# Two gated stages of a hybrid backbone: a weight remainder is computed amid the convolution's taps, and two roots are taken ahead of an evacuation

## The chip, the cores and the metric

One core of a Trainium2 chip runs the whole kernel in one launch. The metric is the device time in microseconds (us) of that core. The engines of the core are TensorE (PE in the rows; PEld are its weight loads), VectorE (DVE), ScalarE (ACT), GpSimd (POOL) and SyncE (SP, which here only issues DMAs). Each runs its own queue of instructions in order, and semaphores tie the queues together.

## The reference, cut to what matters

The program computes two layers of a backbone on 1024 latent and 256 context tokens with 1024 channels. The change touches only the front of layer 0, the gated pointwise unit and the depthwise convolution behind it:

```python
def conformer_conv(h, w_in, b_in, dw_w, dw_b, ln_g, ln_b, w_out, b_out):
    a, gt = jnp.split(h @ w_in + b_in, 2, axis=-1)
    z = a * jax.nn.sigmoid(gt)
    z = depthwise_conv(z, dw_w, dw_b)          # 31 taps, centred
    z = jax.nn.silu(layer_norm(z, ln_g, ln_b))
    return z @ w_out + b_out
...
a = rms_norm(h, norm_g[i, 0]) * (1.0 + sc1) + sh1     # the input, also for context
y = conformer_conv(a, *cm)
h = h + g1 * rms_norm(y, norm_g[i, 1])
```

After it come a gated feed-forward part with a 3-tap convolution, windowed attention and a second feed-forward part.

## The kernel before

Channels lie on the 128 partitions (8 tiles of 128 channels), tokens along the free dimension. Every weight tile of 1024 x 128 is a "unit" of the stream `wstream`. SyncE loads it into `raw`, ScalarE writes its high part `w_hi` (`split` on ScalarE, L496), VectorE the remainder `w_lo = raw - w_hi` (`split` on VectorE, L1001), and TensorE multiplies three times per tile: high by high, high by low, low by high (`unit`, L1729). There are two slots, j = 0 and 1, and two units make a pair q. I write (q,j) for a unit. A unit of the gated stages is 8 tiles x 3 products x 2 halves of the tokens = 48 matmuls.

Two gated phases (`kind == "glu"`) follow each other: pairs 0 to 7 take the first 660 tokens, pairs 8 to 15 the other 620. In each pair, unit (q,0) gives the channel tile `a`, unit (q,1) the gate. ScalarE evacuates the first to `ug` (L645) and the sigmoid of the second to `uv` (L666), VectorE multiplies them into `zA` and `zB` (the product, L1330), which counts `glu_done`. ScalarE may overwrite `ug` only when the product before is done.

Between units TensorE runs adaptive rows, which compute the shifts, scales and gates of both layers: `ada_turn` (L1766) and `ada_rows` (L1758), 16 + 4 short matmuls on a 1 MB slot that GpSimd loads. ScalarE copies each row out (`ada_row_out`, L503).

The order on each engine is written out by hand. For one pair q = q0 + i before the change:

- ScalarE: evacuate (q,0); high part of (q+1,0), which must wait for unit (q,0) since it overwrites its weights; a hosted root, if any; row out; sigmoid of (q,1); high part of (q+1,1); row out.
- VectorE: wait for the sigmoid; product; remainders of (q+1,0) and (q+1,1); then `conv(n)`, the next n operations of the 31-tap depthwise convolution of 8 tiles (L1013, L1015, L1025, L1028, and L1022 that joins even and odd taps), with n from the lists `CONV_A` and `CONV_B`; then the steps of a hosted norm.
- TensorE: unit (q,0), adaptive rows, unit (q,1), adaptive rows. It starts a unit when its remainder is there and its PSUM slot is evacuated.

Each phase hosts a norm of other work. The first hosts the input norm of the second token chunk (`pre`): squares in pair 0, three sums on VectorE behind pair 1's taps (L1040), average on TensorE ahead of unit (3,0) (L1737), root on ScalarE in pair 3 (L514), reciprocal on VectorE behind pair 3's taps (L1044), normalized tiles behind pair 4's (L1070), then high parts and remainders of the activations in pair 7 (L543, L1076). The second hosts the layer norm of the convolution's first 644 outputs (`ln`): sums behind pair 12's taps (L1212, L1208), average ahead of unit (14,0), mean and centring in pair 13 on VectorE (L1217, L1223), squares, sums behind it, average ahead of unit (15,0), root in pair 15, reciprocal behind pair 14's taps, normalized tiles (L1281), silus in pair 15 (L659), high parts and remainders. TensorE, after the first unit of such a pair, waits for the root before it goes on, since the average shares its PSUM banks with the adaptive sums. Behind pair 15 the output projection of the module (`cm`, pairs 16 to 19) runs.

In the loops of VectorE and of this text i counts pairs within a phase. The product of pair q is called product q. On VectorE what the trace shows behind product q up to product q+1 is pair q's share.

Of the kernel before, what the change touches and what calls it, by code (L numbers as in the profile page):

```python
# [37 lines left out]
GA, MIX, HALF, MIX1 = 660, 644, 640, 516  # L38
GB, MIXB = TOK - GA, TOK - MIX
# [3 lines left out]
ZB = ZC + CTX + PAD  # L43
CB = ZC + CTX - PAD
LAG = 5
N_GROUPS = NB * NKV
N_HEADS = N_GROUPS * QPK
CONV_A = (20, 16, 21, 16, 14, 21, 21, 17)
CONV_B = (22, 22, 22, 22, 23, 9, 10, 14)
# [126 lines left out]
def backbone(nc, xT, wstream, adastream, vec, consts, bconsts, rope, out):  # L176
    ph, n_pairs, pair_tiles = plan()
    assert len(pair_tiles) == n_pairs
    with ExitStack() as ctx:
# [305 lines left out]
        def _(act):  # L485
# [26 lines left out]
            def root(s, w, bank=4):  # L512
                act.wait_ge(norm_step, s)
                A(two(rms[:, 0:w], w), misc(w, bank), ACT.Sqrt, bias=eps_t[:]).then_inc(norm_step, 1)  # L514
# [95 lines left out]
            for x in ph:  # L610
                if "hosted" in x:
                    continue
                kind, q0, s, ch = x["kind"], x["q"], x["s"], x.get("chunk")
# [23 lines left out]
                if kind == "glu":  # L637
                    w, host = ch["n"], x["host"]
                    n = host["n"]
                    for i in range(8):  # L640
                        q, g, ga = q0 + i, x["g"] + i, x["ada"] + 2 * i
                        if g:
                            act.wait_ge(glu_done, g)
                        act.wait_ge(unit_done, 2 * q + 1)
                        A(parted(ug[:, 0:w], w), slot(0, w), ACT.Identity, bias=col("cmb_in", i)).then_inc(evacuated, 1)  # L645
                        split(q + 1, 0)
                        if host["kind"] == "pre" and i == 3:
                            root(host["s"] + 5, GB)
                        if host["kind"] == "ln" and i == 6:
                            act.wait_ge(norm_step, host["s"] + 6)  # L650
                            A(t_mix[:], zA[:, :, 0:MIX], ACT.Square).then_inc(norm_step, 1)
                        if host["kind"] == "ln" and i == 7:
                            root(host["s"] + 11, MIX)
                        ada_row_out(ga)
                        if host["kind"] == "ln" and i == 7:
                            for m in range(4):
                                act.wait_ge(in_normed, 4 * n + m + 1)
                                for k in (2 * m, 2 * m + 1):
                                    last = A(t_mix[:, k], zA[:, k, 0:MIX], ACT.Silu, scale=col("ln_g", k), bias=col("ln_b", k))  # L659
                                last.then_inc(in_modulated, 1)  # L660
                        act.wait_ge(unit_done, 2 * q + 2)
                        tiles = t_gb if host["kind"] == "pre" else t_mix
                        if i == 7:
                            for m in range(2):
                                high_part(n, m, tiles[:, 2 * m:2 * m + 2])
                        A(parted(uv[:, 0:w], w), slot(1, w), ACT.Sigmoid, bias=col("cmb_in", 8 + i)).then_inc(evacuated, 1)  # L666
                        if i == 7:
                            for m in range(2, 4):
                                high_part(n, m, tiles[:, 2 * m:2 * m + 2])
                        split(q + 1, 1)  # L670
                        ada_row_out(ga + 1)
                        if host["kind"] == "pre" and i == 0:
                            pre_squares(host)
                        if host["kind"] == "pre" and i in (5, 6):
                            for m in range(2 * (i - 5), 2 * (i - 4)):
                                modulate(n, m, t_gb[:, 2 * m:2 * m + 2], 0, 0, GA)
# [20 lines left out]
                if kind == "wo":  # L697
# [7 lines left out]
                    for v in range(2 * KT):  # L705
                        q, j, u = q0 + v // 2, v % 2, v % KT
# [26 lines left out]
                if kind == "ffn":  # L733
# [4 lines left out]
                    q, p, d = x["q"], x["p"], x["d"]  # L738
                    head, tail, ln, join = x.get("head"), x.get("tail"), x.get("ln"), x.get("join")
                    final = x.get("last")  # L740
                    narrow = head and "narrow" in head
                    for gi, (f0, nf) in enumerate(groups):
# [75 lines left out]
                        q, p = q + nf, p + nf  # L818
# [58 lines left out]
                if kind == "qkv":  # L877
# [19 lines left out]
                    for t in range(30):  # L897
                        q, j = q0 + t // 2, t % 2
# [45 lines left out]
                if kind == "attn":  # L944
# [17 lines left out]
                    for c in range(cuts_by(-1)):  # L962
                        cut(c)
                    for n in range(N_HEADS + LAG):
                        g, hh, m = n // QPK, n % QPK, n - LAG
                        if m >= 0:
# [24 lines left out]
        def _(dve):  # L991
# [3 lines left out]
            def split(q, j):  # L995

                if isinstance(q, int) and q >= n_pairs:
                    return
                dve.wait_ge(hi_ready, 2 * q + j + 1)
                nt = tiles_of_pair(q)  # L1000
                TT(w_lo[:, j, 0:nt], raw[:, j, 0:nt], w_hi[:, j, 0:nt].bitcast(F32), ALU.subtract).then_inc(lo_ready, 1)  # L1001
# [28 lines left out]
            def conv(n):  # L1030

                for op in range(conv_at[0], min(conv_at[0] + n, 2 * KT * (CW + 1))):
                    conv_tap(op // (CW + 1), op % (CW + 1))
                    conv_at[0] = op + 1
# [249 lines left out]
            for x in ph:  # L1284
                if "hosted" in x:
                    continue
                kind, q0, s, ch = x["kind"], x["q"], x["s"], x.get("chunk")
# [25 lines left out]
                if kind == "glu":  # L1313
                    host = x["host"]
                    pre, n, hs = host["kind"] == "pre", host["n"], host["s"]
                    tiles = t_gb if pre else t_mix
                    if pre:
                        parts = [(zA, PAD, 0, GA - 1), (zB, 0, ZB0, GA)]
                        dve.wait_ge(pad_set, 1)
                    else:  # L1320
                        parts = [(zB, GA - ZB0, 0, LAT - GA), (zB, ZC, LAT - GA, GB)]
                    for i in range(8):
                        q = q0 + i
                        if i == 7:
                            split(q + 1, 0)
                            for m in range(2):
                                remainder(n, m, tiles[:, 2 * m:2 * m + 2])
                        dve.wait_ge(evacuated, 2 * q + 2)
                        for z, zo, lo, hi in parts:
                            last = TT(z[:, i, zo:zo + hi - lo], ug[:, lo:hi], uv[:, lo:hi], ALU.mult)  # L1330
                        last.then_inc(glu_done, 1)
                        if i == 7:
                            for m in range(2, 4):
                                remainder(n, m, tiles[:, 2 * m:2 * m + 2])
                        else:
                            split(q + 1, 0)
                        split(q + 1, 1)
                        if not pre and i == 5:
                            ln_mean_out(hs + 4, MIX)
                            ln_centre(hs + 5, zA, MIX)  # L1340
                        if not pre and i == 1:
                            modulation(0, 16, 48, ADA_B, 2)
                        conv((CONV_A if pre else CONV_B)[i])
                        if pre and i == 1:
                            sum_tiles(hs + 1, t_gb)
                        if pre and i == 3:
                            invert(hs + 6, GB)
                        if pre and i == 4:
                            for m in range(4):
                                pre_normed(host, m)  # L1350
                        if not pre and i == 4:
                            assert conv_at[0] >= KT * (CW + 1)
                            ln_first_sum(hs)
                        if not pre and i == 5:
                            sum_tiles(hs + 7, t_mix)
                        if not pre and i == 6:
                            invert(hs + 12, MIX)
                            for m in range(4):
                                ln_normed(hs + 13, zA, MIX, m)
                if kind == "cm":  # L1360
                    for v in range(KT):
                        q, j = q0 + v // 2, v % 2
# [16 lines left out]
                if kind == "wo":  # L1379
# [8 lines left out]
                    for v in range(2 * KT):  # L1388
                        q, j, u = q0 + v // 2, v % 2, v % KT
# [21 lines left out]
                if kind == "ffn":  # L1411
# [4 lines left out]
                    head, tail, ln, join = x.get("head"), x.get("tail"), x.get("ln"), x.get("join")  # L1416
# [4 lines left out]
                    q, p, d = x["q"], x["p"], x["d"]  # L1421
                    for gi, (f0, nf) in enumerate(groups):
# [84 lines left out]
                        q, p = q + nf, p + nf  # L1507
# [57 lines left out]
                if kind == "qkv":  # L1565
# [45 lines left out]
                    for t in range(30):  # L1611
                        q, j = q0 + t // 2, t % 2
# [44 lines left out]
                if kind == "attn":  # L1657
# [11 lines left out]
                    for c in range(cuts_by(-1)):  # L1669
                        cut(c)  # L1670
                    for n in range(N_HEADS + LAG + 2):
                        g, hh, g_out = n // QPK, n % QPK, (n - LAG - QPK - 1) // QPK
                        if g_out >= 0 and (n - LAG - 1) % QPK == 0:
# [424 lines left out]
```

## Time and profile before

| | us |
|---|---|
| median of 3 runs (2950.06 to 2951.52) | 2951.47 |
| the profiled execution's own time | 2953.52 |
| its span from first to last instruction | 2951.70 |
| TensorE matmuls busy, whole span | 2730.4 (93%) |
| VectorE busy, whole span | 2065.3 (70%) |
| ScalarE busy, whole span | 1285.0 (44%) |
| GpSimd busy, whole span | 132.9 (5%) |
| the gated stages, first product to the end of the last remainder | 75 to 409 |

The shares over the whole span are averages over stages of different kinds: the gated stages are a ninth of it. For a change in one stage the busy times of that stage and the waits in it are what to read. In the rows, "[1.75 <-DVE w_lo L1001]" behind an instruction means that its engine was idle for 1.75 us before it and that the named result released it. Instructions of the same line are merged into one row with their count. The time of a merged row can overlap the next row's start by about 0.1 us, so the difference of two starts is the time that an instruction holds its engine.

### The profile page before, as it was taken

The page shows a single profiled execution, that of the slowest core. Times are in us where ns is not written, and L with a number is a line of the kernel's source. Part 1 is how long each engine was busy: PE and PEld are TensorE (multiplying, and loading weights), DVE is VectorE, ACT ScalarE, POOL GpSimd, SP SyncE. Part 2 cuts the span into 40 slices and gives each one's busy share as a digit, 9 for nine tenths or more (in the row PEclk, how much of TensorE's full clock was granted, in tenths as well). Part 3 has the DMA queues.
Part 4 walks back from the last instruction along what each step waited for, and adds up shares of the span by engine and source line. Part 5 has one row for each costly group of instructions (what it writes and reads, how often), then busy time and mean ns, then how long its engine had stood idle before and what let it go on. Part 6 is the DMA issues. An engine that isn't in the chain of part 4 may idle for free. (4 is left out here: it accounts for less than half of the span.)

```text
span 2951.7 us, 45016 instructions
## 1 busy us (share of the span) xinstructions
PE 2730.4 (93%) x17388; PEld 2462.6 (83%) x17388; DVE 2065.3 (70%) x2897; ACT 1285.0 (44%) x1910; POOL 132.9 (5%) x177
## 2 busy tenths in 40 slices
PE   5898877999999989999999989998999999999996
PEld 4787776999998979999997767776889989778785
DVE  3899988889877367556667767665577457584665
ACT  3232244433436353333443557776453334443333
POOL 0000000000000000000000003333000000000000
PEclk7999988999999989999999989999999999999998
DMA  6444432233232212222222220000222232333322
GB/s 266 147 153 157 143 114 96 69 91 92 75 89 69 72 58 78 87 93 78 86 79 93 79 72 1 2 1 2 79 85 88 92 100 86 100 103 111 100 93 85
DMA packets 66519, 263.14 MB, mean 89 GB/s; under 512 B 6960, under 2 KB 7216, under 8 KB 60080
## 3 DMA queue, kind: packets, MB, share of 16 engines
q1 hardware_dynamic: 58368, 213.17, 22.9%
q0 software_dynamic: 5760, 41.95, 4.1%
q10 hardware_dynamic: 2224, 5.69, 0.6%
q8 instruction: 118, 1.93, 0.3%
q14 instruction: 49, 0.40, 0.0%
HBM read 256.58 MB, written 4.19 MB: 88 GB/s over the span
## 5 line engine op out<-in xcount | busy, mean ns | idle before, releaser
L1729 PE MATMUL PS<-a_hi,w_hi 128*128 128x322 f32 (+7 forms) x3584 | 919.5, 325 | 72.6 <-DVE a_lo L1076 37.5
L1729 PE MATMUL PS<-a_lo,w_hi 128*128 128x322 f32 (+7 forms) x3584 | 899.4, 320 | 0.0
L1729 PE MATMUL PS<-a_hi,w_lo 128*128 128x322 f32 (+7 forms) x3584 | 898.6, 319 | 0.0
L1729 PEld LDWEIGHTS PS<-a_hi,w_hi 128*128 128x128 f32 x3584 | 613.0, 192 | 125.8 <-issue 47.5
L1729 PEld LDWEIGHTS PS<-a_lo,w_hi 128*128 128x128 f32 x3584 | 615.3, 192 | 26.7 <-issue 4.8
L1729 PEld LDWEIGHTS PS<-a_hi,w_lo 128*128 128x128 f32 x3584 | 612.7, 192 | 24.4
L1001 DVE TENSOR_TENSOR w_lo<-raw,w_hi 128x1024 fp32r<-128x1024 f32 (+2 forms) x380 | 443.7, 1171 | 190.9 <-ACT w_hi L496 186.9
L496 ACT ACTIVATE w_hi<-raw 128x1024 fp32r<-128x1024 f32 (+2 forms) x380 | 386.3, 1017 | 0.3 <-DMA raw<-wstream 0.2
L1729 PE MATMUL PS<-z_hi,w_hi 128*128 128x320 f32 (+1 forms) x1056 | 301.2, 340 | 30.1 <-DVE z_lo L1426 27.9
L1729 PE MATMUL PS<-z_hi,w_lo 128*128 128x320 f32 (+1 forms) x1056 | 298.7, 337 | 0.0
L1729 PE MATMUL PS<-z_lo,w_hi 128*128 128x320 f32 (+1 forms) x1056 | 298.6, 337 | 0.0
L1729 PEld LDWEIGHTS PS<-z_hi,w_hi 128*128 128x128 f32 x1056 | 185.0, 189 | 49.0 <-DVE z_lo L1426 32.3
L1432 DVE TENSOR_SCALAR cgv<-u_both,vec_sb 128x512 f32<-128x512 f32 (+1 forms) x132 | 74.6, 565 | 200.7 <-ACT u_both L811 124.5
L1729 PEld LDWEIGHTS PS<-z_hi,w_lo 128*128 128x128 f32 x1056 | 185.0, 189 | 13.9
L1729 PEld LDWEIGHTS PS<-z_lo,w_hi 128*128 128x128 f32 x1056 | 185.1, 189 | 13.5
L1441 DVE SCALAR_TENSOR_TENSOR cgv<-u_both,vec_sb,cgv 128x383 f32<-128x383 f32 (+2 forms) x220 | 149.0, 694 | 52.9 <-ACT cgv L750 49.6
L480 POOL TENSOR_SCALAR prob<-prob,soft 128x640 f32<-128x640 f32 (+1 forms) x128 | 110.2, 876 | 1447.3 <-DVE soft L1705 1447.3
L746 ACT ACTIVATE z_hi<-cgv 128x640 fp32r<-128x640 f32 (+3 forms) x88 | 60.5, 688 | 229.9 <-DVE cgv L1505 229.9
L1450 DVE SCALAR_TENSOR_TENSOR cgv<-u_both,vec_sb,cgv 128x383 f32<-128x383 f32 (+3 forms) x220 | 149.0, 694 | 7.8 <-DVE cgv L1441 6.1
L856 ACT ACTIVATE u_both<-PS 128x640 f32<-128x640 f32 (+1 forms) x80 | 53.1, 664 | 227.3 <-PE PS L1729 227.3
L1682 DVE TENSOR_REDUCE soft<-PS 128x1 f32<-128x640 f32 (+1 forms) x128 | 101.3, 791 | 56.5 <-PE PS L1972 55.8
L811 ACT ACTIVATE u_both<-PS 128x644 f32<-128x644 f32 (+3 forms) x88 | 57.5, 653 | 171.5 <-PE PS L1729 171.5
(248 smaller groups left out, 3138.1 us busy)
## 6 DMA issues: line engine op xcount, KB each, us to landing
raw<-wstream SPq DMA_DIRECT2D x380, 512.0 KB, 3.6
ada_slot<-adastream POOLq DMA_DIRECT2D x40, 1024.0 KB, 5.2
ada_first<-adastream SPq DMA_DIRECT2D x4, 2048.0 KB, 20.4
h<-xT SPq DMA_DIRECT2D x1, 2640.0 KB, 15.5
h<-xT ACTq DMA_DIRECT2D x1, 2480.0 KB, 12.4
out<-h ACTq DMA_DIRECT2D x1, 2048.0 KB, 9.3
out<-h SPq DMA_DIRECT2D x4, 512.0 KB, 2.8
rope_sb<-rope ACTq DMA_DIRECT2D x1, 1024.0 KB, 5.1
```

Source lines behind the costliest of these rows:

```text
L480: nc.gpsimd.tensor_scalar(pr, pr, soft[:, 4, g % 2, hh:hh + 1], 1.0, ALU.mult, ALU.mult).then_inc(prob_scaled, 1)
L496: A(w_hi[:, j, 0:nt], raw[:, j, 0:nt], ACT.Copy).then_inc(hi_ready, 1)
L746: A(z_hi[:, ds(i, 1), 0:n_out], cv[:, 0:n_out].unsqueeze(1), ACT.Copy).then_inc(zh_done, 1)
L811: last = A(parted(uv[:, 0:w], w), slot(1, w), ACT.Copy)
L856: A(dst, slot(j, n_out), ACT.Copy).then_inc(evacuated, 1)
L1001: TT(w_lo[:, j, 0:nt], raw[:, j, 0:nt], w_hi[:, j, 0:nt].bitcast(F32), ALU.subtract).then_inc(lo_ready, 1)
L1432: TS(dst[:, 0:n_out], u[:, 0:n_out], col(f"cw{l}", f * 4 + 1), col(f"cw{l}", f * 4 + 3), ALU.mult, ALU.add).then_inc(mid, 1)
L1441: last = STT(dst[:, lo:hi], u[:, lo - 1:hi - 1], left, dst[:, lo:hi], ALU.mult, ALU.add)
L1450: last = STT(dst[:, lo:hi], u[:, lo + 1:hi + 1], right, dst[:, lo:hi], ALU.mult, ALU.add)
L1682: nc.vector.reduce_max(soft[:, 0, g % 2, hh:hh + 1], PS[:, 2 * (hh % 2):2 * (hh % 2) + 2, :].rearrange("p a b -> p (a b)")[:, 0:w], AX_X). ...
L1729: last = MM(PS[:, 2 * j + m, 0:n], wt[:, j, k, :], mv[:, k, m * n:(m + 1) * n], start=(k == 0 and p_ == 0), stop=(k == tiles - 1 and p_ == 2))
```

## The change

On VectorE, the remainder of the next pair's first unit is no longer computed behind the product. In pair q it is that of (q+2,0), one pair further ahead, and it stands behind the first seven operations of the pair's share of the convolution (`AHEAD`), with the rest of the share behind it. To start this off, the remainder of (1,0) stands ahead of product 0. The last pair of the second phase has none, as pair 14 has already made that of (16,0). In pair 7 and 15 the remainder that stood at the top of the pair falls away likewise. The remainder of (q+1,1) stays behind the product.

On ScalarE, the two hosted roots of pairs 3 and 15 stand ahead of the evacuation of that pair's first unit, and no longer behind the high part of (q+1,0).

No arithmetic, tile, load or semaphore changes; the order of the counts `lo_ready` stays (q,0), (q,1), (q+1,0).

```diff
+AHEAD = 7
...
@@ ScalarE, kind == "glu"
+                        if host["kind"] == "pre" and i == 3:
+                            root(host["s"] + 5, GB)
+                        if host["kind"] == "ln" and i == 7:
+                            root(host["s"] + 11, MIX)
                         if g:
                             act.wait_ge(glu_done, g)
                         act.wait_ge(unit_done, 2 * q + 1)
                         A(parted(ug[:, 0:w], w), slot(0, w), ACT.Identity, bias=col("cmb_in", i)).then_inc(evacuated, 1)
                         split(q + 1, 0)
-                        if host["kind"] == "pre" and i == 3:
-                            root(host["s"] + 5, GB)
...
-                        if host["kind"] == "ln" and i == 7:
-                            root(host["s"] + 11, MIX)
@@ VectorE, kind == "glu"
+                        if pre and i == 0:
+                            split(q + 1, 0)
                         if i == 7:
-                            split(q + 1, 0)
                             for m in range(2):
                                 remainder(n, m, tiles[:, 2 * m:2 * m + 2])
...
                             for m in range(2, 4):
                                 remainder(n, m, tiles[:, 2 * m:2 * m + 2])
-                        else:
-                            split(q + 1, 0)
                         split(q + 1, 1)
...
-                        conv((CONV_A if pre else CONV_B)[i])
+                        taps = (CONV_A if pre else CONV_B)[i]
+                        conv(min(taps, AHEAD))
+                        if pre or i < 7:
+                            split(q + 2, 0)
+                        conv(max(taps - AHEAD, 0))
```

## Rows read from the trace of the kernel before

**Rows 1.** Table of windows, the gated stages; its columns stand in its first line.
```profile
core 0: us, PE busy (x) PEld busy (x) DVE busy (x) ACT busy (x) POOL busy (x), PEclk, DMA share, GB/s
75.00:388.00 313.00, 267.72 (x1987) 245.99 (x1979) 301.43 (x368) 87.08 (x116) 15.60 (x29) 0.94 0.43 148
```
**Rows 2.** Waits of VectorE, 75 to 390 us: total us, times, longest.
```profile
DVE zA L1330 <- ACT u_both L666: 23.4, 3, 16.7
DVE rms L1044 <- ACT rms L514: 2.0, 1, 2.0
DVE zB L1330 <- ACT u_both L666: 0.7, 1, 0.7
DVE a_lo L1076 <- ACT a_hi L543: 0.2, 1, 0.2
```
**Rows 3.** Waits of TensorE for weight remainders, 75 to 390 us.
```profile
PE PS L1729 <- DVE w_lo L1001: 26.9, 13, 4.6
```
**Rows 4.** VectorE in order of time: start, us, line, operation; products 0 to 3.
```profile
75.46 0.85 DVE L1330 TENSOR_TENSOR zA<-u_both 128x659 f32<-128x659 f32 x1 [16.68 <-ACT u_both L666]
...
76.33 2.36 DVE L1001 TENSOR_TENSOR w_lo<-raw,w_hi 128x1024 fp32r<-128x1024 f32 x2
78.60 0.61 DVE L1013 TENSOR_SCALAR acc<-zA,vec_sb 128x644 f32<-128x644 f32 x1
...
79.59 0.88 DVE L1025 SCALAR_TENSOR_TENSOR acc<-zA,vec_sb,acc 128x644 f32<-128x644 f32 x1
...
94.94 0.85 DVE L1330 TENSOR_TENSOR zA<-u_both 128x659 f32<-128x659 f32 x1 [0.87 <-ACT u_both L666]
...
115.51 0.84 DVE L1330 TENSOR_TENSOR zA<-u_both 128x659 f32<-128x659 f32 x1
...
141.36 0.84 DVE L1330 TENSOR_TENSOR zA<-u_both 128x659 f32<-128x659 f32 x1 [5.84 <-ACT u_both L666]
```
**Rows 5.** ScalarE in order of time: high part in pair 1, root in pair 3.
```profile
86.00 1.05 ACT L496 ACTIVATE w_hi<-raw 128x1024 fp32r<-128x1024 f32 x1
...
125.31 0.81 ACT L645 ACTIVATE u_both<-PS,vec_sb 128x660 f32<-128x660 f32 x1 [9.67 <-PE PS L1729]
...
128.38 0.78 ACT L514 ACTIVATE rms<-PS,eps_t 128x620 f32<-128x620 f32 x1
```
**Rows 6.** TensorE in order of time: starts of units (1,0), (1,1), (3,0), and averages.
```profile
77.60 0.57 PE L1729 MATMUL PS<-a_hi,w_hi 128*128 128x330 f32 x2 [1.75 <-DVE w_lo L1001]
...
86.47 0.42 PE L1729 MATMUL PS<-a_hi,w_hi 128*128 128x330 f32 x1
...
115.64 1.31 PE L1737 MATMUL PS<-t_gb,cst 128*128 128x310 f32 x4 [0.74 <-DVE t_gb L1040]
117.64 0.57 PE L1729 MATMUL PS<-a_hi,w_hi 128*128 128x330 f32 x2 [0.68 <-DVE w_lo L1001]
...
352.30 2.52 PE L1737 MATMUL PS<-t_mix,cst 128*128 128x322 f32 x4 [6.17 <-DVE t_mix L1208]
```
**Rows 7.** Table of windows, TensorE alone: busy us (count), granted clock, DMA.
```profile
352.30:357.00 4.70, 4.70 (x17) 0.62 0.28 91
```
**Rows 8.** VectorE, TensorE and ScalarE in order of time, pairs 14 and 15.
```profile
373.81 0.86 DVE L1330 TENSOR_TENSOR zB<-u_both 128x364 f32<-128x364 f32 x2
...
387.02 4.18 DVE L1044 RECIPROCAL rms<-rms 128x644 f32<-128x644 f32 x1 [2.00 <-ACT rms L514]
...
375.86 0.56 PE L1729 MATMUL PS<-a_hi,w_hi 128*128 128x310 f32 x2 [0.56 <-DVE w_lo L1001]
...
383.83 1.05 ACT L496 ACTIVATE w_hi<-raw 128x1024 fp32r<-128x1024 f32 x1
```
**Rows 9.** The projection's first unit on TensorE, its first two evacuations on ScalarE.
```profile
415.10 0.89 PE L1729 MATMUL PS<-a_hi,w_hi 128*128 128x322 f32 x2
...
425.03 0.80 ACT L602 ACTIVATE zA<-PS,vec_sb 128x644 f32<-128x644 f32 x1 [10.85 <-PE PS L1729]
...
432.16 0.80 ACT L602 ACTIVATE zA<-PS,vec_sb 128x644 f32<-128x644 f32 x1 [4.61 <-PE PS L1729]
```

## The prediction, written before the result was known

> **What bounds the kernel now.** The change touches only the sixteen pairs of the two gated stages, so I first looked at the table of windows for the stretch in which they run up to the last reciprocal, 75 to 388 us [rows 1]. VectorE is busy 301.43 of 313 us, TensorE 267.72. That already says which engine has no room. The list of VectorE's waits in it [rows 2] sums to 26.3 us, of which 16.7 us is the wait ahead of the very first product, when there are no taps yet. TensorE's waits look larger: 26.9 us in 13 waits for a weight remainder [rows 3]. They tempt one to take them as the prize of this change. But such a wait ends when VectorE gets round to the remainder, and VectorE gets round to it when its taps are through. Moving work inside VectorE's queue does not shorten that queue. What counts is the time in which VectorE stands still, and what new standstills the new order makes.
>
> Where does it stand still? 0.87 us ahead of product 1 and 5.84 us ahead of product 3 [rows 4] (with the 16.68 us they are the 23.4 us of rows 2), 0.7 us ahead of product 9, 0.2 us ahead of a remainder of the activations, and 2.0 us ahead of the second reciprocal: 0.87 + 5.84 + 0.7 + 0.2 + 2.0 = **9.6 us**. Behind that reciprocal come normalized tiles, silus, high parts and remainders in the same order as before the change, so that tail and all later stages move with it. VectorE's work between product 0 (75.46 us) and the reciprocal is the same before and after: the remainder of (1,0), 1.13 us, leaves the stretch (it stands ahead of product 0 now, in the 16.7 us of idle time), and the remainder of (16,0), 1.13 us, enters it. So the difference of the two kernels is the new waits less 9.6 us.
>
> **Part 1: the root ahead of the evacuation.** In pair 3 ScalarE evacuates unit (3,0) at 125.31 us, cuts the high part and only then takes the root, which ends at 129.16 us [rows 5], 3.85 us after the unit; TensorE waits for it, and VectorE's product 3 comes late by that. After the change the average is done long before unit (3,0) ends, so the root and its table load lie beside that unit. Nobody is queued behind the moved root but the evacuation, and that waits for the unit anyway. It costs nothing; its cover is the 9.67 us in which ScalarE waits for that unit [rows 5]. Alone it would take out most of the 5.84 us (141.36 - 3.85 is 137.5 us, and the half-speed stretch behind TensorE's stall goes too, so some 136 us, where VectorE is through at 135.5), and the same edit in pair 15 the 2.0 us ahead of the reciprocal. Together some 7 us, by itself.
>
> **Part 2: the remainder amid the taps.** The remainder of (q+2,0) now stands behind seven taps of pair q, and the whole VectorE queue stands behind its wait for the high part, which ScalarE cuts only when unit (q+1,0) has ended and is evacuated. Prices: a product with its edge 76.33 - 75.46 = 0.87 us, a remainder (78.60 - 76.33) / 2 = 1.13 us, the two first taps 0.99 us, each other tap (94.94 - 0.87 - 79.59) / 18 = 0.80 us [rows 4]; from the start of a unit to its cut high part 86.00 + 1.05 - 77.60 = 9.45 us, from unit to unit 86.47 - 77.60 = 8.87 us, adaptive rows included [rows 5, 6]. Now the queue step by step.
>
> Pair 0: the unit (1,0) has its remainder early and starts when the adaptive rows are issued, 1.8 us earlier, at 75.8 us and not at 77.60 (its wait for the remainder is 1.75 us, rows 6). Its high part is ready at 85.25 us. VectorE is through product, remainder (1,1) and seven taps at 75.46 + 0.87 + 1.13 + 4.99 = 82.45 us. New wait **2.8 us**; the 0.87 us is gone.
>
> Pair 1: product at 94.94 - 0.87 + 2.8 = 96.9 us. Unit (2,0) starts two units after 75.8, at 93.5, high part at 103.0. VectorE needs it at 96.9 + 0.87 + 1.13 + 7 x 0.80 = 104.5 us. No wait, with 1.5 us to spare. The host's three sums end at 115.51 + 1.9 = 117.4 us.
>
> Pair 2: TensorE is now ahead but the average must wait for those sums. It has been idle some 6 us by then. At full clock the average takes 1.31 us and unit (3,0) starts at 118.8; the high part is ready at 128.2. VectorE arrives at 117.4 + 0.87 + 1.13 + 5.6 = 125.0. Wait 3.2 us. But in pair 14 an average after 6.17 us of idle time took 2.52 us [rows 6], 1.2 us more, and over the 4.7 us from its start the granted clock was 0.62 of full speed [rows 7], so part of it ran at the lower of the two levels, 1.2 and not 2.4 GHz; 0.38 of 4.7 us is 1.8 us lost. By that row the wait becomes some 5.0 to 5.2 us. Bounds 3.2 and 5.2; I take **5.2 us**, since the idle time is nearly the same.
>
> The Trainium skill ("TensorE: Matmul & The Clock Gate", What's actually happening) says that an idle array passes half the clock pulses until it has been busy again. The trace agrees: the average behind the long pause took 2.52 us and the one behind a short pause 1.31 [rows 6]. By the page alone a unit of 48 matmuls that ran wholly at 1.2 GHz would be about twice as long, by an estimate 13 us for 48 times 330 columns.
>
> Pairs 3 to 13: product 3 at 117.4 + 20.0 + 5.2 = 142.6 us. From here VectorE's 20 us a pair (115.51 to 135.52 us in pair 2) exceed the 17.7 us that TensorE needs for two units (2 x 8.87 us), so TensorE runs ahead until it waits for the remainder of (q,1). Then unit (q+1,0) starts about 11.3 us and its high part is ready 20.8 us after product q-1, while VectorE asks for it at 20 + 7.6 = 27.6 us. No wait. The 0.2 and 0.7 us vanish too.
>
> Pair 14: the average follows the sums at S = 373.8; unit (15,0) starts at S + 1.4 (the average, 1.31 us) and its high part is ready at S + 10.4 (383.83 + 1.05 - 375.86 = 9.0 us after its start, rows 8). VectorE is at the cut at S + 0.8 + 1.13 + 7 x 0.81 = S + 7.6. New wait **2.8 us**, against the 2.0 us of before [rows 8]. So what the root gives here is taken back.
>
> **The sum.** 2.8 + 5.2 + 2.8 = 10.8 us of new waits less 9.6 us of old ones: +1.2 us; with the full clock at pair 2 it is -0.8 us. Above that: unit (15,0) could also fall into the lower clock (1.8 us by rows 7), and TensorE's last gated unit now ends some 10 us earlier, so that it enters the projection after a longer pause. There the first unit's evacuation begins 9.9 us after the unit, the second's 7.1 us after the first's [rows 9]; a second unit like the first would cost 2.8 us. I take nothing for both: before has a pause and a slow unit at the same place. My own case reaches from -1.5 to +5 us.
>
> The profiled execution took 2953.52 us for a span of 2951.70 us, the median of the three runs is 2951.47 us. The sum is a difference of chains within the span and applies to the median as it stands: 2951.5 + 1.2 = 2952.7 us.
>
> **Rivals.** *Faster, TensorE's waits are the prize:* if the remainders' waits were ended by the order alone and not by VectorE's load, the 26.9 us would go: 2924.6 us. Against it stands the VectorE that is busy 96% of the stretch. Milder: the three mid-tap waits don't arise because the units end sooner than I replay them; then the full 9.6 us is gained, 2942 us. It needs high parts 2.8, 5.2 and 2.8 us earlier at three places. Both together 12%.
>
> *Slower, the wait among the taps recurs:* TensorE now pauses ahead of each second unit, and where the lower clock stretches a first unit by more than the spare time (1.5 us at pair 1, some 2.5 us at pair 3, some 7 us in the steady state) VectorE stops again with all its taps behind it. At the lower level 330 columns last 330 / 1.2 GHz = 0.275 us, at the upper (125.31 - 117.64) / 48 = 0.16 us [rows 5, 6], so a unit wholly at the lower one costs 48 x 0.115 = 5.5 us. One such unit in a thin place puts it at 2951.5 + 1.2 + 5.5 = 2958.2 us or more; below 1.5 us of stretch it costs nothing. Against it: the stretch after the longest pause in rows 6 and 7 lost 1.8 us, not 5.5. 10%.
>
> *The edit moves nothing that counts,* VectorE being full: between -0.8 and +1.2 us, which is my own case and can't be told from it by time.
>
> **Chances.** About 0.2%, 5.9 us, is what a measurement of this kernel can tell from no change. My case lies within it but for its edge: 78%. Faster by more 12%, slower by more 10%. The range goes from 2944 us (most of the milder gain) to 2958 us; some 9% lie on either side of it.
>
> **What would show each step.** VectorE's waits for w_hi in the gated stages: three, of about 2.8, 5.2 and 2.8 us, near 82, 125 and 382 us, and none elsewhere; no wait for rms in the two reciprocals; TensorE waiting ahead of each second unit, not each first; the second reciprocal within 2 us of 387 us. I am wrong if VectorE waits among the taps in the steady pairs, or if it doesn't wait in pairs 0, 2 and 14, or if the projection starts later by more than the reciprocal does.

## The result and the profile after

| | before | after |
|---|---|---|
| median, 16 runs each | 2951.40 us | 2955.66 us |
| the profiled execution's own time | 2953.52 us | 2954.21 us |
| its span | 2951.7 us | 2952.4 us |
| product 0 to the second reciprocal, in the profile | 75.46 to 387.02: 311.56 us | 74.42 to 389.51: 315.09 us |

The ratio is 1.0016, 95% interval 1.0009 to 1.0023: the changed kernel is 4.3 us slower (2.7 to 6.8 us by the interval). The difference is clear of noise, and within the 0.2% that I had called "no change". The spans of the two profiled executions differ by only 0.7 us, because in the changed one the first product came 1.04 us earlier (unit (0,1) ran 8.33 us there and 9.11 us in the other), and because 1.8 us more came back behind the second reciprocal, which is told under "The account over all of them". The stretch from product 0 to the second reciprocal, where the change lies, is 3.53 us longer.

The table of windows of the changed kernel, 75 to 388 us, answers [rows 1]: VectorE is busy for 3 us less, TensorE for 5 us more, at a lower granted clock (0.91 and not 0.94).

```profile
75.00:388.00 313.00, 272.57 (x2002) 252.28 (x2002) 298.42 (x366) 87.56 (x117) 15.84 (x30) 0.91 0.44 147
```

The waits of VectorE, and of TensorE its longest and those for a remainder, in the changed kernel, 75 to 390 us (engine, line waited for, total us, times, longest), answer [rows 2 and 3]. The 11.3 us are again the wait ahead of product 0.

```profile
DVE w_lo L1002 <- ACT w_hi L497: 12.5, 5, 5.3
DVE zA L1332 <- ACT u_both L667: 11.3, 1, 11.3
DVE rms L1218 <- PE PS L1741: 0.7, 1, 0.7
...
PE PS L1741 <- DVE t_mix L1209: 13.5, 1, 13.5
PE PS L1733 <- DVE w_lo L1002: 9.9, 5, 3.3
```

All five of the old waits of VectorE are gone: no wait for the sigmoid after product 0, none for a root. TensorE's waits for a remainder fell from 26.9 to 9.9 us, a gain of 17 us if one goes by that list, and the kernel became slower. For the most part they moved: TensorE now comes early and waits for other results of VectorE, 13.5 us ahead of the average of pair 14 (before 6.2 us), 8.9 us for the activations of pair 8 (1.6 us) and 6.2 us ahead of the average of pair 3 (0.7 us). On VectorE stand 12.5 us of new waits for a high part. In the order of time on VectorE (start, us, line, operation, idle time and what ended it):

```profile
84.29 1.23 DVE L1002 TENSOR_TENSOR w_lo<-raw,w_hi 128x1024 fp32r<-128x1024 f32 x1 [2.71 <-ACT w_hi L497]
...
129.37 1.23 DVE L1002 TENSOR_TENSOR w_lo<-raw,w_hi 128x1024 fp32r<-128x1024 f32 x1 [5.30 <-ACT w_hi L497]
...
233.26 1.23 DVE L1002 TENSOR_TENSOR w_lo<-raw,w_hi 128x1024 fp32r<-128x1024 f32 x1 [0.24 <-ACT w_hi L497]
...
250.20 1.23 DVE L1002 TENSOR_TENSOR w_lo<-raw,w_hi 128x1024 fp32r<-128x1024 f32 x1 [0.18 <-ACT w_hi L497]
...
385.95 1.23 DVE L1002 TENSOR_TENSOR w_lo<-raw,w_hi 128x1024 fp32r<-128x1024 f32 x1 [4.11 <-ACT w_hi L497]
```

The two averages on TensorE and the table of windows from the start of each show why the second (5.30 us) and the last (4.11 us) are that long: both averages took the time of the lower clock level, as the one in [rows 6 and 7] did.

```profile
116.52 2.43 PE L1741 MATMUL PS<-t_gb,cst 128*128 128x310 f32 x4 [6.18 <-DVE t_gb L1041]
...
374.32 2.51 PE L1741 MATMUL PS<-t_mix,cst 128*128 128x322 f32 x4 [1.95 <-DVE t_mix L1041]
```
```profile
116.50:127.00 10.50, 10.48 (x50) 9.76 (x51) 7.56 (x10) 0.78 (x1) 0.00 (x0) 0.76 0.18 51
...
374.30:379.00 4.70, 4.68 (x18) 3.89 (x19) 4.70 (x7) 0.86 (x2) 0.00 (x0) 0.66 0.86 302
```

Behind the gated stages the chain only shifted. The tail ahead of the projection kept its steps (here the wait for the high parts is 3.63 us where before had 2.53 us, as the remainder of (16,0), 1.13 us, no longer lies in it), and the adaptive turns ahead of the projection come 2.44 us later in this trace, 409.91 and not 407.47 us; with the 1.04 us by which the stretch began earlier that is 3.5 us. TensorE's longer pause there, 16.0 and not 7.5 us, cost nothing: from the last turn to the first evacuation it took 426.90 - 416.67 = 10.2 us, as against 425.03 - 414.23 = 10.8 us.

### The profile page after: what moved, and what is told of

Read it like the earlier page. It is cut to its first block and busy times, and to the rows that moved or that the text cites. A ratio compares the mean times of both kernels' runs of the same rounds, so it can differ in the third digit from the quotient of the medians.

```text
span 2952.4 us, 45016 instructions
## 1 busy us (share of the span) xinstructions
PE 2725.2 (92%) x17388; PEld 2460.2 (83%) x17388; DVE 2065.3 (70%) x2897; ACT 1282.2 (43%) x1910; POOL 132.1 (4%) x177
## 5 line engine op out<-in xcount | busy, mean ns | idle before, releaser
L1733 PEld LDWEIGHTS PS<-a_hi,w_lo 128*128 128x128 f32 x3584 | 612.5, 192 | 24.4
L1733 PE MATMUL PS<-z_hi,w_hi 128*128 128x320 f32 (+1 forms) x1056 | 301.4, 340 | 30.0 <-DVE z_lo L1430 27.9
```

The lines of the kernel that those rows point to most:

```text
L1733: last = MM(PS[:, 2 * j + m, 0:n], wt[:, j, k, :], mv[:, k, m * n:(m + 1) * n], start=(k == 0 and p_ == 0), stop=(k == tiles - 1 and p_ == 2))
```

## The experiments

All compare with the kernel before, measured beside them on the same chip. The theory throughout: VectorE is full in the gated stages, so the time is its work plus the time in which it stands still, and each part of the change is worth the standstills that it removes less those that it makes.

### The roots alone

```diff
+                        if host["kind"] == "pre" and i == 3:
+                            root(host["s"] + 5, GB)
+                        if host["kind"] == "ln" and i == 7:
+                            root(host["s"] + 11, MIX)
                         if g:
                             act.wait_ge(glu_done, g)
...
```

> The kernel before with one part of the change alone: the two hosted roots stand ahead of the evacuation of unit (3,0) and (15,0), the remainders stay where they were. Theory (VectorE's standstills set the time, and the roots are the part that pays): of before's 9.6 us of waits ahead of the second reciprocal, the 5.84 us ahead of product 3 and the 2.0 us ahead of the reciprocal go, 0.87 + 0.7 + 0.2 us stay. 2951.4 - 7.8 = 2943.6 us, range 2941 to 2946, ratio 0.9974. Rival (the roots hide nothing, since TensorE and not VectorE is the bound, and after its 4 us stalls it would wait for the remainder anyway): no change, 2951. Second rival (the moved root delays ScalarE's evacuation and costs by itself what the whole change lost): slower than 2951.

Measured: 2947.05 us against 2950.99 us, ratio 0.9986 (0.9977 to 0.9995). Faster, so the rivals fall, but about half of the 7.8 us. The waits of VectorE ahead of products 4 and 6 in its trace, 1.34 and 1.33 us, tell where a part went. The first:

```profile
156.60 0.85 DVE L1330 TENSOR_TENSOR zA<-u_both 128x659 f32<-128x659 f32 x1 [1.34 <-ACT u_both L666]
```

The waits of 5.84 and 2.0 us are gone as expected, 0.86 and 0.71 us stayed, and these two, 2.67 us, are new. Ahead of the first of them unit (4,0) had started behind a pause of 2.14 us and ran in part at the lower clock (table of windows: 0.83 over 137 to 147 us). Units (4,0) and (6,0), behind pauses of 2.14 and 1.95 us, took 9.07 and 9.11 us; in the kernel before, behind pauses of 1.68 and 1.96 us, they took 7.58 us each, 1.5 us less, and products 4 and 6 waited for nothing. The stretch is 306.09 us, 5.5 us shorter than before's. TensorE's waits for remainders are 26.0 us here, nearly the 26.9 us of before: they are no measure of the time.

### The remainder alone

The changed kernel with both roots put back behind the high part.

> The changed kernel with its roots put back behind the high part: the other part alone, remainder of (q+2,0) behind seven taps. Theory: the waits among the taps of pairs 0, 2 and 14 stay (2.7, 5.3, 4.1 us in the changed kernel), pair 3 gets one more of about 1.7 us, since TensorE again waits for the root before unit (3,1); at the reciprocal the root's delay of some 3.9 us lies beside the wait and the remainder and three taps behind it (1.1 + 2.4 us) and costs nothing more. So 13.2 + 1.7 - 9.6 = 5.3 us over before: 2956.7 us, range 2954 to 2960. Rival (remainder ahead of time helps TensorE, the loss comes from the roots): at or below 2951.

Measured: 2959.06 us against 2950.99 us, ratio 1.0027 (1.0016 to 1.0038). That is 8.1 us where I had expected 5.3 us, within the range. The loss comes from the remainder's place, and the roots made up for a part of it. The waits behind product 0 are near those expected, 4.45 and not 5.3 us in pair 2, with one more, 2.40 us ahead of product 3, that I had not listed: 2.71 + 4.45 + 2.40 + 2.04 + 0.69 + 4.12 = 16.4 us. The wait of 2.04 us in pair 3 follows a unit (3,1) of 9.02 us, which had started behind TensorE's stop of 4.00 us for the root; other units of that stage took 7.60 us. These are three of them, in the order of time:

```profile
130.27 1.22 DVE L1002 TENSOR_TENSOR w_lo<-raw,w_hi 128x1024 fp32r<-128x1024 f32 x1 [4.45 <-ACT w_hi L497]
145.09 0.85 DVE L1332 TENSOR_TENSOR zA<-u_both 128x659 f32<-128x659 f32 x1 [2.40 <-ACT u_both L667]
...
154.97 1.23 DVE L1002 TENSOR_TENSOR w_lo<-raw,w_hi 128x1024 fp32r<-128x1024 f32 x1 [2.04 <-ACT w_hi L497]
```

### Twelve and three operations ahead of the remainder

```diff
-AHEAD = 7
+AHEAD = 12
```

> The changed kernel with 12 operations of the convolution ahead of the remainder of (q+2,0), not 7. Both parts of the change stay. Theory (the loss is the wait for a high part that comes too late for the seventh tap; five more taps are 4.0 us of cover): the waits of 2.7, 0.24 and 5.3 us shrink to 0, 0 and 1.3 us; pair 14 has only 10 operations, so its 4.1 us shrink by 2.4 us to 1.7 us or less; the 0.7 us ahead of the mean copy stay. 3.7 us of waits, 13.2 - 3.7 = 9.5 us less than the changed kernel (2955.7): 2946.2 us, and down to 2943 us where the clock keeps its upper level. Rival (the loss is the slower clock of TensorE, which has longer pauses now, and not the place of the remainder): the time stays at 2955 to 2956 us, as the pauses stay.

Measured: 2946.56 us against 2950.99 us, ratio 0.998 (0.9971 to 0.9989), where the changed kernel had 1.0016. The list of waits of VectorE, 64 to 410 us, with 3.1 us in 2 where the changed kernel has 12.5 us in 5:

```profile
DVE w_lo L1002 <- ACT w_hi L497: 3.1, 2, 1.7
```

> The changed kernel with 3 operations ahead of the remainder of (q+2,0), not 7. Theory: every wait grows by the four taps of 0.8 us that no longer cover it, 3.2 us in each of pairs 0, 2 and 14, and pairs 7 and 8 get waits of 1 to 3 us: 9.6 + 1.5 to 3 = some 11 to 13 us over the changed kernel, 2967 to 2969 us. The steady pairs stay free, as they had some 7 us to spare. Rival (slower clock, not the place): unchanged at 2955 to 2956. Rival (thin margins: the wait recurs in most pairs): 2985 or more, 3.2 us in ten more pairs.

The edit is `AHEAD = 3`. Measured: 2969.17 us against 2950.99 us, ratio 1.0062 (1.0048 to 1.0075). Its list of waits:

```profile
DVE w_lo L1002 <- ACT w_hi L497: 23.7, 6, 7.7
```

Of its waits 5.91, 7.65 and 5.86 us stand in pairs 0, 2 and 14, which is 3.2, 2.35 and 1.75 us more than with seven, 3.00 us in pair 7, 0.19 us in pair 8 and 1.11 us in pair 13. Pairs 2 and 14 rose by less than the 3.2 us of the four operations, as TensorE was faster there than in the changed kernel: unit (3,0) took 8.32 and not 9.17 us, and the average ahead of unit (15,0) ran at the full clock although TensorE had paused longer ahead of it (TensorE in order of time):

```profile
385.17 1.35 PE L1741 MATMUL PS<-t_mix,cst 128*128 128x322 f32 x4 [3.32 <-DVE t_mix L1041]
```

With 3, 7 and 12 operations the time goes 2969.2, 2955.7, 2946.6 us: the place sets the loss. The rival of the slower clock alone falls, for with twelve the granted clock over 75 to 412 us is 0.90, as it is with seven (0.90), and before has 0.93. The rival of thin margins falls too: pairs 3 to 6 and 9 to 12 stayed free even with three.

### The same kernels with a VectorE that has room

In each, eight of the 31 taps of a channel tile work on 32 columns, for the first nine of the 16 tiles; the rest of these taps is left out:

```diff
                     src, tap = z[:, t:t + m], col("dw_w", k % KT * CW + t)
+                    if k < 9 and 22 <= t < 30:
+                        src, even, odd = src[:, 0:32], even[:, 0:32], odd[:, 0:32]
```

> The kernel before, but of each channel tile's taps in the gated stages eight (of 31) work on 32 columns and not on 644 or 651: that part of the convolution is left out. Some 0.7 us of VectorE's work go for each of them, 72 in all, some 50 us, while every instruction, wait and count stays. It asks what bounds the stages once VectorE has room. Theory (VectorE's load hid what its order costs): only a part of the 50 us comes back as time, since now product, remainder and unit follow each other in a ring: 2 x 8.87 us of TensorE plus 1.75 us of waiting for the remainder, 19.5 us a pair, against 20 to 21 us so far. Some 14 us faster, 2937 us (2932 to 2942), and VectorE waits for the sigmoid in most pairs. Rival (VectorE's load alone sets the time, with no ring): 40 us or more faster, 2911 us or less.

Measured: 2945.87 us against 2951.28 us, ratio 0.9977 (0.9968 to 0.9986). VectorE's busy time fell by 45.4 us over the whole span and by 40.2 us in the stretch, less than the 50 us that I had put down, and 5.4 us of time went with it. Theory right in kind, wrong in size: I had expected 14 us, and the result lies outside my range. The waits of VectorE, 64 to 390 us:

```profile
DVE zA L1332 <- ACT u_both L666: 41.9, 7, 17.7
DVE zB L1332 <- ACT u_both L666: 11.3, 3, 4.5
DVE a_lo L1078 <- ACT a_hi L543: 5.4, 1, 5.4
DVE rms L1046 <- ACT rms L514: 2.0, 1, 2.0
```

Less the 17.72 us ahead of product 0 VectorE now stands still for 42.9 us in the stretch. Now the ring of sigmoid, product, remainder and unit is what ends last. Products 1 and 2 stand 19.48 us apart (97.14 to 116.62), as worked out, but products 0 and 1, 3 and 4, and 4 and 5 stand 21.0 us apart, with a granted clock of 0.91 in 78 to 97, 0.92 in 142 to 163 and 0.91 in 163 to 183 us (1.00 in 97 to 116 us); I had reckoned with the full clock throughout, and with a reciprocal, sums and normalized tiles that fit into the ring.

> The changed kernel with the same eight narrow taps in each tile (that part of the convolution is left out). Theory: here the change does what it is for, as the first unit of a pair no longer waits for product and remainder; what is left are waits among the taps of 2 to 3 us in half of the pairs. Some 16 to 20 us faster than the kernel before with the same narrow taps, 2919 us (2914 to 2925). Rival (the order of the remainder is worth nothing on this chip, whatever VectorE's load): within 5 us of the kernel before with narrow taps, 2932 to 2942 us.

Measured: 2921.33 us, ratio 0.9898 (0.9883 to 0.9913). Against the kernel before with the same narrow taps that is 24.5 us less, more than the 16 to 20 us expected, because that kernel was slower than I had thought; the 2919 us themselves were met. The rival falls. The same edit that costs 4.3 us where VectorE is full gives 24.5 us where it is not.

> The changed kernel with 12 operations ahead of the remainder, and the same eight narrow taps in each tile (left out as above). Theory: with shorter taps in front, the wait among the taps is shorter still than with 7: some 5 to 7 us faster than the changed kernel with narrow taps, 2913 us (2908 to 2919). Rival (a later remainder now delays TensorE's next unit, since VectorE's load no longer covers it): 2 us or more slower than the changed kernel with narrow taps, 2921 us or more.

Measured: 2912.80 us, ratio 0.9872 (0.9857 to 0.9887), 8.5 us less than with seven. The remainder behind twelve operations does not come too late for TensorE even here.

### Three places mended

Twelve operations ahead, and in addition:

```diff
                         if i == 7:
+                            if not pre:
+                                split(q + 1, 0)
...
+                        if pre and i == 1:
+                            sum_tiles(hs + 1, t_gb)
                         conv(min(taps, AHEAD))
-                        if pre or i < 7:
+                        if pre or i < 6:
                             split(q + 2, 0)
                         conv(max(taps - AHEAD, 0))
-                        if pre and i == 1:
-                            sum_tiles(hs + 1, t_gb)
```

> The kernel with 12 operations ahead of the remainder, and mended at its last places: the three sums of the hosted norm in pair 1 stand ahead of that pair's taps, so that TensorE need not pause for the average, and the remainder of (16,0) stands behind the normalized tiles in pair 15, as in the kernel before, so that nothing waits ahead of the reciprocal. Theory (VectorE's standstills up to the reciprocal set the time): waits of 1.4 and 1.7 us go and 1.1 us of work leaves the stretch, 4.2 us less than with 12 alone (2946.6 us in its run): 2942.4 us, 2940 to 2945. Rival (what is left is noise of the clock and no more can be had here): 2946 to 2947.

Measured: 2940.74 us against 2951.28 us, ratio 0.9966 (0.9954 to 0.9978): within the range, so the rival falls. It is faster than both kernels of this document, and below the kernels with the roots alone (0.9986) and with twelve alone (0.998), by intervals that only just overlap. Its list of VectorE's waits, 64 to 390 us, has nothing in the stretch but the 0.7 us ahead of the mean; the 11.5 us are ahead of product 0 and 2.5 us in the tail. The average of pair 3 now runs without a pause, in 1.31 us.

```profile
DVE zA L1334 <- ACT u_both L667: 11.5, 1, 11.5
DVE a_lo L1077 <- ACT a_hi L544: 2.5, 1, 2.5
DVE rms L1218 <- PE PS L1743: 0.7, 1, 0.7
...
110.61 1.31 PE L1743 MATMUL PS<-t_gb,cst 128*128 128x310 f32 x4
```

### The account over all of them

For each kernel the stretch from product 0 to the second reciprocal, VectorE's waits in it added up from its order of time, and the difference of the two, which is work:

| kernel | stretch | waits | work | stretch less before's | median less before's |
|---|---|---|---|---|---|
| before | 311.6 | 9.7 | 301.9 | | |
| after | 315.1 | 13.2 | 301.9 | +3.5 | +4.3 |
| roots alone | 306.1 | 4.2 | 301.9 | -5.5 | -3.9 |
| remainder alone | 318.3 | 16.4 | 301.9 | +6.8 | +8.1 |
| twelve ahead | 305.2 | 3.8 | 301.4 | -6.4 | -4.4 |
| three ahead | 326.5 | 24.4 | 302.1 | +15.0 | +18.2 |
| three places mended | 300.9 | 0.7 | 300.2 | -10.7 | -10.5 |
| narrow taps, before | 304.5 | 42.8 | 261.7 | -7.0 | -5.4 |
| narrow taps, after | 281.1 | 19.7 | 261.3 | -30.5 | -30.0 |
| narrow taps, twelve ahead | 270.7 | 9.6 | 261.1 | -40.9 | -38.5 |

That the work comes out the same is the finding. The kernel with three places mended has 300.2 us, 1.1 us of it less since the remainder of (16,0) has left the stretch. In the six kernels above it the work is the same within 0.8 us, in the three with narrow taps within 0.6 us, and in both groups the waits alone make the difference. With full taps the medians follow within 3.2 us, with narrow ones within 2.4 us. A single profiled execution has its own clock states, and before's lies 2.1 us above its median, 2953.52 and not 2951.40 us. From the second reciprocal to the last one of the program the traces of all six other kernels with full taps gain on it, by 0.8 to 3.4 us (the changed kernel from 2.49 us behind it to 0.70 us), the kernel with the roots alone too, whose remainders stand where before's do. Before's three medians differ by 0.4 us.

## Why the prediction was right, point by point

**What bounds the stages: right, and shown.** The account above is the argument of the prediction, and it holds for ten kernels. TensorE's 26.9 us of waits for remainders were not the prize: with 9.9 us the kernel was slower, with 26.0 us (the roots alone) it was faster.

**The old waits go: right.** All 9.6 us (9.7 us, as the wait that I had taken as 0.2 us was 0.25 us) vanished, and work stayed at 301.9 us.

**Pair 0: 2.8 us expected, 2.71 us measured. Pair 1: none, and none. Pair 2: 5.2 us expected, bounds 3.2 and 5.2, and 5.30 us measured,** with an average of 2.43 us behind a pause of 6.18 us, as in the row that I had taken for it. Reading the price from the nearest pause, and not from the average at the same place in the trace of before (1.31 us), was worth 2 us. That it came within 0.1 us is partly luck: behind the same pause of 6.18 us the kernel with the remainder alone had a unit (3,0) of 8.31 us, and not 9.17 us as here, and waited 4.45 us. **Steady pairs: none, and all but none:** 0.24 us in pair 7 and 0.18 us in pair 8, as unit (8,0) came late behind a pause of 8.9 us for activations and ran for 9.57 us. I had given no thought to those pairs.

**Pair 14: 2.8 us expected, 4.11 us measured. This is the term that was mis-sized.** I had taken 1.31 us for the average since TensorE's pause ahead of it was short. The pause was as short as before's (1.95 and 1.88 us), and yet the average took 2.51 us and the unit 7.94 us, where before had 1.35 and 7.19 us. I had named this case (1.8 us by rows 7) and set it at nothing. With the full clock the term was right: in the kernel with three ahead average and unit (15,0) took 1.35 and 7.34 us, and its wait of 5.86 us less the four operations (3.2 us) is 2.6 us. In the kernel with the remainder alone the average took 1.35 us but the unit behind it 8.84 us, and the wait was 4.12 us. It is the mechanism of my slower rival, a stretch at the lower clock in a place without spare time, on a small scale. **The mean copy waited 0.69 us,** which I had left out: the remainder of (14,0) no longer lies between the product and it, so that it comes before the average, which at the lower clock took 2.51 us, has ended.

**The sum.** 2.8 + 5.2 + 2.8 = 10.8 us were 2.71 + 5.30 + 0.24 + 0.18 + 0.69 + 4.11 = 13.23 us, and +1.2 us became +3.5 us in the trace and +4.3 us in the median. The sign, the range of 2944 to 2958 us and the case "within 0.2%" held, at the upper half: 4.3 us of 5.9 us. The upper bound of +5 us of my own case had room for the term that moved (1.8 us) and for a second slow unit at the projection (2.8 us); with both it should have been 5.8 us. The second did not come: TensorE was through with the gated stages some 6 us earlier and not 10 (at 393.91 and not at 399.93 us), and from the last adaptive turn to the first evacuation it took 10.2 us as against 10.8 us.

**The signs.** Two that I had named did not come as written. The second reciprocal began at 389.51 us, 2.5 us behind 387.02 us and not within 2 us. And TensorE was to wait ahead of each second unit: its five waits for a remainder, 9.9 us, do all stand ahead of a second unit, but only of pairs 6, 7, 11, 12 and 13. Its longer pauses were elsewhere, 13.5 us ahead of the average of pair 14 and 8.9 us ahead of unit (8,0).

**The roots.** Some 7 us by themselves was too much: 3.9 us in the median, 5.5 us in the trace, as products 4 and 6 waited 2.67 us for units that ran 1.5 us longer, at the lower clock. I had judged the roots from the two waits that they remove, and not asked what is late next.

**The rivals.** That the waits among the taps don't arise is what twelve operations ahead show, for the most part: 2946.6 us, where the prediction had 2942 us for that case; the mended kernel reached 2940.7 us. The slower rival (the wait recurs in steady pairs) came in the changed kernel with 0.42 us, in pairs 7 and 8. Its mechanism shows elsewhere: 2.04 us in pair 3 with the remainder alone (2959.1 us), 3.00 and 1.11 us in pairs 7 and 13 with three ahead. The rival of a full gain of 26.9 us needs a VectorE that has room: with narrow taps the changed order gave 24.5 us.

**Left open.** Why TensorE ran the average ahead of unit (15,0) at the lower clock in the changed kernel and not in the kernel before, with nearly equal pauses (1.95 and 1.88 us), is not settled: no run here separates what TensorE did before that pause from the moment at which the pause fell. The length of the pause alone doesn't decide it, for in four other kernels the same average followed pauses of 2.59 to 3.32 us and took 1.35 to 1.40 us. That the medians exceed the traces (by 0.7 us for the changed kernel, 3.2 us with three ahead) fits how far the profiled executions lie from their medians (2.1 us above for before, 1.5 and 1.4 us below for those two), but no second trace was taken.

## What to carry to other kernels

Before you pay for a waiting engine, ask whether the engine that it waits for is full: if that one's queue sets the time, only that one's standstills count, and a wait that you put into the middle of its queue holds up everything behind it. Place such a step behind enough independent work that its input is ready even in the first pairs, when the pipeline has not filled yet: seven operations were enough for the steady pairs but for 0.4 us, and the loss came from three places at the start and the end. When a large wait is removed, look for what is late next, and price each step behind a pause by its slow form.

## What the runs showed of the hardware that I had not expected

The same average of four matmuls behind the same pause of 1.9 us took 1.35 us in one kernel and 2.51 us in another, so that one step off the path of the busy engine had two prices, 1.2 us apart. After pauses of 2.6 to 3.3 us it took 1.35 to 1.40 us in four kernels, and the average of pair 3 after one of 3.18 us took 2.43 us; after pauses of 6.2 us (four kernels) an average took 2.4 to 2.5 us each time. Units show the same: in the kernel before with narrow taps six units (q,0) of the first phase followed pauses of 1.67 to 1.75 us, and two of them took 7.6 us, the other four 9.1 us. A unit behind a pause of 8.9 us took 9.57 us, one that followed at once 7.20 us. The pause of 16.0 us ahead of the projection cost no more than the one of 7.5 us, since both ended at the lower clock and the first unit took 9.9 us before its evacuation (from 415.10 to 425.03 us) in the kernel before and 9.4 us (from 417.54 to 426.90 us) in the changed one.
